# Mean squares of eleven heads from high and low parts: two float32r products with ones in place of one native fp32 product

## The reference

```python
def head_rmsnorm(o, g):
    B, S, H, dv = o.shape
    y = o * lax.rsqrt(jnp.mean(o * o, axis=-1, keepdims=True) + EPS)
    return (y * g.astype(jnp.float32).reshape(H, dv)).reshape(B, S, H * dv)
...
    y_h = head_rmsnorm(o_h, g_hg_norm[l]) * jax.nn.silu(hg.astype(f32))
    y_g = head_rmsnorm(o_g, g_gla_norm[l]) * jax.nn.silu(gr.astype(f32))
    y = jnp.concatenate([y_h, y_g], axis=-1).astype(h.dtype)
    h = h + y @ w_out[l]
```

## Time and profile before

| | us |
|---|---|
| median of 3 runs | 2427.51 |
| lowest, highest | 2427.02, 2428.92 |
| the profiled execution, its own time | 2428.29 |
| its span, first to last instruction | 2426.6 |

### The profile page before, as it was taken

How to read it: one execution, slowest core, us unless ns; L and a number is a source line. 1 busy time by engine, 2 the same in 40 slices (tenths; PEclk the granted TensorE clock), 3 DMA queues, 4 the chain that set the end, 5 groups by cost and what they waited for, 6 DMA issues and landing times.

```text
span 2426.6 us, 34798 instructions
## 1 busy us (share of the span) xinstructions
PE 2393.7 (99%) x13375; PEld 2082.1 (86%) x13375; DVE 1939.1 (80%) x2589; ACT 1202.9 (50%) x1787; POOL 50.7 (2%) x79
## 2 busy tenths in 40 slices
PE   8999999999999999999999999999999999999997
PEld 6888888888777888999999999988888888888885
DVE  6777777788887447988888888899999999995456
ACT  6445444444445235666666666643333333345345
POOL 4000000000000000000000000000000000000111
PEclk9999999999999999999999999999999999999999
DMA  6323323333324234666666666697564575633322
GB/s 176 87 73 82 86 70 85 87 84 81 79 74 152 92 131 137 182 204 200 199 197 196 197 196 196 205 353 253 198 232 160 191 257 195 229 131 116 112 85 99
DMA packets 381406, 373.71 MB, mean 154 GB/s; under 512 B 5532, under 2 KB 311352, under 8 KB 379224
## 3 DMA queue, kind: packets, MB, share of 16 engines
q1 hardware_dynamic: 381240, 371.88, 48.0%
q10 hardware_dynamic: 32, 0.01, 0.0%
HBM read 304.76 MB, written 67.11 MB: 153 GB/s over the span
## 4 chain that ended last, share of the span: by engine, by line
PE 62%; DVE 4%; ACT 1%; issue 1%; DMA 1%; DVEq 0%; ACTq 0%; SPq 0%
PE bank L2323 20%; PE bank L2325 20%; PE bank L2324 20%; DVE w_lo L2064 1%; DMA ring<-in_w_down 0%; DVE h L2110 0%; DVE w_lo L1927 0%; ACT w_hi L1143 0%; DVE w_lo L2201 0%; PE bank L2708 0%; PE bank L2603 0%; DVE gate_e L2227 0%; DVE h L2230 0%; PE bank L2401 0%; ACT gate_inv L1355 0%
## 5 line engine op out<-in xcount | busy, mean ns | idle before, releaser
L2323 PE MATMUL bank<-u_hi,w_hi 128*128 128x512 f32 x896 | 361.8, 404 | 3.4 <-DVE w_lo L1466 2.0
L2323 PE MATMUL bank<-w_hi,forms 128*128 128x512 f32 x896 | 349.4, 390 | 1.1 <-DVE h L2110 1.1
L2325 PE MATMUL bank<-u_hi,w_lo 128*128 128x512 f32 x896 | 349.8, 390 | 0.0
L2324 PE MATMUL bank<-u_lo,w_hi 128*128 128x512 f32 x896 | 349.2, 390 | 0.0
L2325 PE MATMUL bank<-w_hi,forms 128*128 128x512 f32 x896 | 348.7, 389 | 0.0
L2324 PE MATMUL bank<-w_lo,forms 128*128 128x512 f32 x896 | 348.6, 389 | 0.0
L2323 PE MATMUL bank<-xs,w_hi 128*128 128x256 f32 x1024 | 289.9, 283 | 1.4 <-DVE w_lo L1927 0.9
L2324 PE MATMUL bank<-xs,w_hi 128*128 128x256 f32 x1024 | 289.6, 283 | 0.0
L2325 PE MATMUL bank<-xs,w_lo 128*128 128x256 f32 x1024 | 289.5, 283 | 0.0
L1273 ACT ACTIVATE w_hi<-ring 128x1024 fp32r<-128x1024 f32 x124 | 132.0, 1066 | 214.6 <-PE bank L2325 140.4
L1466 DVE TENSOR_TENSOR w_lo<-w_raw,w_hi 128x2048 fp32r<-128x2048 f32 x70 | 160.0, 2286 | 63.2 <-ACT w_hi L874 63.0
(11 more groups left out here) (315 smaller groups left out, 5235.1 us busy)
## 6 DMA issues: line engine op xcount, KB each, us to landing
w_raw<-in_w_in SPq DMA_DIRECT2D x56, 1024.0 KB, 5.6
forms_scratch<-stage SPq DMA_DIRECT2D x32, 1792.0 KB, 11.4
forms<-forms_scratch SPq DMA_DIRECT2D x56, 1024.0 KB, 8.3
ring<-in_w_down SPq DMA_DIRECT2D x39, 1024.0 KB, 5.3
w_raw<-in_w_up SPq DMA_DIRECT2D x32, 1024.0 KB, 7.8
raw<-in_w_up SPq DMA_DIRECT2D x32, 1024.0 KB, 8.0
w_raw<-in_w_down SPq DMA_DIRECT2D x25, 1024.0 KB, 5.1
ring<-in_w_pg SPq DMA_DIRECT2D x18, 1024.0 KB, 5.0
```

Source lines behind the costliest of these rows:

```text
L2323: pe.matmul(ps, whi, xhi, start=start, stop=False, skip_group_check=shared)
L2324: pe.matmul(ps, whi, xlo, start=False, stop=False, skip_group_check=shared)
L2325: return pe.matmul(ps, wlo, xhi, start=False, stop=stop, skip_group_check=shared)
```

## The change

For heads 0 to 10 the squares are split as the weights are. A new ScalarE step, `square_parts`, copies the squares to a float32r tile `square_hi` (in the place of `norm[:, 1]`); a new VectorE step, `square_rest`, writes `square_lo` = squares - `square_hi` (in the place of `norm[:, 2]`). TensorE then waits for `osq_lo` in place of the squares, and makes two float32r products with the ones. The last head keeps its two plain products, and all other users of the ones read the same bits as float32.

```diff
+            def square_parts(hd):
+
+                if hd.gla:
+                    act.wait_ge(osq_ready, hd.h + 1)
+                else:
+                    act.wait_ge(osq_ready_hg, hd.h + 1)
+                act.activation(square_hi, norm[:, 0, :], ACT.Copy).then_inc(osq_hi, 1)
...
                 if prev:
                     square_o(prev)
+                    if not prev.gla:
+                        square_parts(prev)
                 else:
                     slot(2)
                 if hd.gla:
                     silu(hd, "conv", 0)
+                    if prev.gla:
+                        square_parts(prev)
                 else:
                     forget_gate(hd)
...
+            def square_rest(hd):
+
+                v.wait_ge(osq_hi, hd.H + 1)
+                v.tensor_tensor(square_lo, norm[:, 0, :], square_hi.bitcast(F32), ALU.subtract).then_inc(osq_lo, 1)
...
                     conv(hd, 0, kk[:], hd.h + 4)
                     if prev.gla:
                         square_sum(prev)
+                    else:
+                        square_rest(prev)
                     apply_silu(hd, "conv", 0, kk[:], also=kk_back[:, :, :])
+                    if prev.gla:
+                        square_rest(prev)
                     evacuate(hd.unit(1), conv_in[:, CONV - 1:])
                 elif prev:
-                    forget_gate(hd)
+                    forget_gate(hd, lambda: square_rest(prev))
...
-                if hd.gla:
-                    pe.wait_ge(osq_ready, hd.h + 1)
-                else:
-                    pe.wait_ge(osq_ready_hg, hd.h + 1)
-                pe.matmul(bank[3][:, :], ones[:, :], norm[:, 0, :], start=True, stop=True).then_inc(norm_ps, 1)
+                pe.wait_ge(osq_lo, hd.H + 1)
+                pe.matmul(bank[3][:, :], ones_r[:, :], square_hi, start=True, stop=False)
+                pe.matmul(bank[3][:, :], ones_r[:, :], square_lo, start=False, stop=True).then_inc(norm_ps, 1)
```

More of the change, by code:

```diff
@@ L177, in build @@
         ident = sb("ident", [P, P])
-        ones = sb("ones", [P, P])
+        ones_r = sb("ones", [P, P], F32R)
+        ones = ones_r[:, :].bitcast(F32)
         vec1 = sb("vec1", [P, P])
@@ L223, in build @@
         ez = mx("ez", [P, S])
+        norm_at = nc.sbuf_base
         norm = mx("norm", [P, 3, S])
@@ L239, in at @@
             return nc.alloc_sbuf_tensor_at(name, shape, dt, offset=offset)
+        norm_parts = at("norm_parts", norm_at, [P, 3, S], F32R)
+        square_hi, square_lo = norm_parts[:, 1, :], norm_parts[:, 2, :]
         h = at("h", region1 + KT * D, [P, KT, S])
@@ L326, in build @@
         decay01_ready, cross_exp, cross_ready = sem("decay01_ready"), sem("cross_exp"), sem("cross_ready")
+        osq_hi, osq_lo = sem("osq_hi"), sem("osq_lo")
         o_done, osq_act, osq_ready, osq_ready_hg, norm_ps = (
```

## The result

| | us |
|---|---|
| before, median of 22 runs (lowest, highest) | 2427.67 (2426.96, 2429.65) |
| changed, median of 22 runs (lowest, highest) | 2432.02 (2430.65, 2434.15) |
| ratio, 95% interval | 1.0017 (1.0011 to 1.0023) |
| changed, profiled execution: own time, span | 2430.84, 2429.0 |

The change makes the kernel 4.3 us slower. The sign and the mechanism of the waits came out, but the forecast is 2.2 us short of the median, and that part is the more instructive one. One execution of the kernel before beside experiments 9 to 12 took 2633 us at a mean granted clock of 0.85, where all others beside the experiments have 0.994 or more, and is left out.

What follows compares the result with a forecast made beforehand. TensorE, busy for 99% of the span at full clock, was taken as the bound, tied to VectorE at a few places. -0.66 (HGRN2 heads and head 7's sum) + 2.95 (GLA heads) = +2.3 us on 2427.5 gave 2429.8, range 2426.4 to 2432.9.

Steps and rivals of the forecast that it cites:

- Term 1: Sum matmuls on TensorE: two float32r products take 0.45 us for 0.86, saving 0.41 a head, 4.5 for eleven.
- Term 2: New copy (0.62 us) and subtraction (0.68) in HGRN2 heads fit in idle time of ScalarE and VectorE: cost 0.
- Term 3: HGRN2 heads: VectorE's chain to level 1 holds heads 0 to 5, saving 0; with heads 6 and 7, -0.66 us.
- Term 5: GLA heads: TensorE's old waits for VectorE at 575.85 and 596 vanish in heads 9 and 10's iterations, returning 1.22 us each.
- HGRN2 saving kept: Rival, chance 0.15: HGRN2 heads keep their matmul saving, another 2.6 us less, 2427.2.
- Term 4: GLA heads 8 to 10: subtraction stands behind the key's silu, so TensorE waits; taken alone, stalls of 2.31, 2.54 and 2.32 us.
- nothing is given back: Rival, chance 0.15: VectorE is held up as well, the old waits stay, stalls stand alone: +5.3 us, 2432.8.
- the clock's term: Rival, chance 0.02: the clock falls to 1.2 GHz at GLA stalls, 11 us more each, up to 33 in all, 2463.
- The prediction's own sign: Stated sign of being wrong: a head behind a stall runs at a lower granted clock.

Runs made afterwards that it cites:

- experiment 9: Kernel before, with eight throw-away matmuls on TensorE ahead of its wait at the output projection: 2427.45 us.
- Experiment 10: Changed kernel with eight throw-away matmuls ahead of each of four waits (three GLA squares' low parts, output projection): 2429.46 us, ratio 1.0007 to the kernel before.
- experiment 11: Kernel of experiment 5 plus eight throw-away matmuls ahead of the wait at the output projection: 2423.33 us, ratio 0.9983.
- experiment 12: Kernel of experiment 5 with the first output weights split earlier, ahead of levels 4 and 5 in the last head: 2423.81 us.
- experiment 4: Changed kernel, with the GLA heads' copy and subtraction moved ahead of the key's silu: 2427.84 us, ratio 0.9998.
- experiment 6: Kernel before, no split, with level 0's operands and the exponentials of levels 0 and 1 made earlier in HGRN2 heads: 2427.49 us, ratio 1.0002.
- experiment 2: Split sums in HGRN2 heads alone, GLA heads as in the kernel before: 2427.63 us against 2428.73, ratio 0.9997.
- experiment 5: Split sums in HGRN2 heads alone, plus level 0's operands and the exponentials of levels 0 and 1 made earlier: 2424.72 us against 2427.6, ratio 0.9986.
- experiment 3: Split sums in GLA heads 8 to 10 alone, HGRN2 heads as in the kernel before: 2432.02 us, ratio 1.0016.
- experiment 8: The changed kernel run again unchanged, on the chip of experiments 5 to 7: 2432.01 us, ratio 1.0016.
- experiment 7: Changed kernel with the GLA heads' subtraction 2.9 us later on VectorE, behind the low part of unit 3's weights: 2445.03 us, ratio 1.0073.

## Why the prediction was right, and where it was short

**Terms 1 and 2 held.** The two products with ones start 0.23 apart (experiment 4: 547.83, 548.06), and copy and subtraction take 0.63 and 0.68; no idle time of TensorE in an HGRN2 head is for them.

**Term 3 held.** The sums of the HGRN2 heads lie 52.59 apart in both kernels (94.52 to 410.07 in the changed one), so the 0.41 saved went into waiting. The new wait at level 1 is printed as 0.26; with the 0.25 by which printed idle times fall short (Term 5) it is 0.51, of which the kernel before had some 0.09 (experiment 6). Forecast -0.66 in all; read from the starts, head 6 saves 0.24 where 0.25 was said and head 7 0.46 where 0.41 was said, which makes -0.70, and experiment 2 measures -0.5 to -1.0. The rival "HGRN2 saving kept" (2427.2) falls by the same wait, and experiments 5 and 6 show it from the other side: with the chain shortened the saving comes out.

**Term 4 was near.** With the 0.25 added the stalls are 2.25, 2.26 and 1.74, against 2.31, 2.29 and 2.02. The third is shorter because VectorE was delayed less behind the second stall than the 0.61 a head that Term 5 took: from TensorE's arrival at head 8's sum, its subtractions stand 0.38 and 0.66 us later than the evacuation did before, so head 9 added 0.28.

**Term 5 held in kind.** Both old waits went, in the two iterations named, and the one at the output projection is still 1.9. Counted from TensorE's arrival at head 8's sum, it came 0.60, 1.18 and 2.51 us late to the sums of heads 9 and 10 and to the output projection, where +0.68, +1.34 and +2.95 were forecast. From the program's first sum to the output projection the queue lost 1.84 us in the profiled execution, against the +2.3 of the sum. The rival "nothing is given back" gave 2432.8, close to the median of 2432.02, but its mechanism isn't there: the waits that it keeps are gone. Experiment 10 puts the queue's loss at 2.0, and at the time 2429.46, 0.3 under the forecast.

**What failed is the clock's term.** The prediction gave it a chance of 0.02 and priced a fall at 11 us a stall, and took it that a wait of 1.9 us has no fall behind it, because the one trace had none. All three were wrong. Behind waits of about 2 us the clock fell in part of the executions; the kernel before has a fall at its wait of 1.90 (17 of 33 executions, 9 of 27 and 9 of 32 on three chips, and none of eleven once it is filled). And a fall costs 1.6 us, not 11 (groups of the kernel before: 2429.2 - 2427.6, 2428.8 - 2427.2, 2428.9 - 2427.4). The changed kernel has three stalls of 1.5 to 2.0 us beside that wait, and with the four filled it is 2432.0 - 2429.5 = 2.5 us faster: some one and a half falls in an execution. That is the 2.2 us which the forecast missed and the 0.3 by which its queue was too long. The prediction's own sign, a head behind a stall at a lower clock, came in experiment 3.

How often each of the four waits has its fall was not counted over all executions. The three traces with all four (the changed kernel, experiments 3 and 8) have one at the output projection each, one of the three behind the first and behind the second stall, and none behind the third, the shortest.

**Where the error came from.** One profiled execution, without a fall, was taken for all, though the three runs shown lay at 2427.02, 2427.51 and 2428.92, a step of 1.4 to 1.9 that fits one fall (their clocks are not known). And the earlier trace rows could not carry the argument, nor the reading that the clock is full "in every slice": a slice is 61 us and 9 is anything from 0.9 up. The kernel before itself stood at 0.50 from 2417 to its end, when TensorE had no more work, and its last slice reads 9; experiment 7's page, with a clock of .995 and the second block below, reads 9 in all slices.

```profile
2417.00:2418.00 1.00, 0.00 (x0) 0.00 (x0) 0.97 (x2) 1.00 (x1) 0.00 (x0) 0.50 0.00 0
2418.00:2419.00 1.00, 0.00 (x0) 0.00 (x0) 0.80 (x2) 0.22 (x2) 0.00 (x0) 0.50 0.14 57
```

```profile
553.00:554.00 1.00, 1.00 (x3) 0.82 (x4) 0.00 (x0) 0.00 (x0) 0.00 (x0) 0.50 0.55 126
554.00:555.00 1.00, 1.00 (x4) 0.80 (x3) 0.96 (x2) 0.24 (x1) 0.00 (x0) 0.50 1.09 319
```

## What to carry to other kernels

An engine that is busy for 99% may still be tied to another at every head: before an instruction is made cheaper, ask at the next place where TensorE takes a result of VectorE whether there is slack, and read a small growth of a group's duration there as a wait. Here the edit in the HGRN2 heads gives 0.5 to 1.0 us alone and 3.9 with one block of work moved. Where the kernel is full, a wait of some 2 us on TensorE can have a second price behind it; read the granted clock in windows of 1 us behind each wait, and compare the steps between executions with it, in more than one of them.

## What the runs showed of the hardware

- After waits of about 2 us TensorE's granted clock fell to half in some executions of one and the same program and not in others: starts of 128x512 products 0.43 apart against 0.23, cost 1.6 us by the times and 1.7 by the windows. The Trainium skill, "TensorE: Matmul & The Clock Gate", Part 1, lists two states of this clock, idle at 1.2 GHz and busy at 2.4 GHz; the windows agree (0.50 and 1.00, with mixed ones at the edges).
- The length of a wait alone does not say whether the clock falls: behind 1.90 at the output projection it did in experiment 8 and did not in the kernel before, and the wait of 4.04 us for the first product of the kernel before has none behind it.
- In a wait of 5.02 us it fell before the wait was over: experiment 7's window 635 to 640 is at 0.50 throughout, and its first product starts at 636.80.
- The fall need not begin with the first product behind the wait: in experiment 8 it began with the fourth, at 758.65, in experiment 3 with the first, at 550.59.
- Throw-away products in a wait kept the clock up: the 33 executions of experiments 9, 10 and 11 all have a mean clock of .998.
